# Late queries of branch A projected later, and every other lookup of the first token tile weighed by DVE

## What is computed

```python
n = rms_norm(h, norm1_g) * (1.0 + scale1) + shift1
h = h + gate1 * hybrid_mixer(n)        # three token mixers A, B, C, gated, merged, times w_out
n = rms_norm(h, norm2_g) * (1.0 + scale2) + shift2
h = h + gate2 * peer_ffn(n)            # per token 8 heads x 16 looked-up experts
```

```python
q = rms_norm(q, q_gain); k = rms_norm(k, k_gain)      # q = n @ w_in[:, aq], per head of 64
logits = einsum('bqhd,bqkd->bqhk', q, k_sel) * scale  # k_sel: the top 128 keys by an indexer
p = softmax(where(valid, logits, -inf)); out = einsum('bqhk,bqkd->bqhd', p, v_sel)
```

```python
u = u_tab[expert]; vv = v_tab[expert]                 # 1024 floats each
act = gelu(einsum('nd,nhkd->nhk', xb, u)); out = einsum('nhk,nhkd->nd', g * act, vv)
```

## Time and profile before

| | us |
|---|---|
| median of 3 runs | 2057.0 (2055.41 to 2059.61) |
| the profiled execution | 2055.41 |
| its span, first to last instruction | 2053.6 |
| PE busy | 1667.6 (81%) |
| DVE busy | 1454.6 (71%) |
| ACT busy | 576.0 (28%) |
| POOL busy | 633.5 (31%) |
| DMA moved | 658.7 MB, of which 536.9 MB by the lookups |

### The profile page before, as it was taken

One profiled execution on the slowest core, in us unless ns is written; L12 is line 12 of the kernel. 1 busy time (PEld: TensorE's weight loads), 2 busy tenths in 40 slices (PEclk: granted clock), 3 DMA queues, 4 the chain that ended last, 5 costly groups with the idle time before them and its releaser, 6 DMA issues.

```text
span 2053.6 us, 17698 instructions
## 1 busy us (share of the span) xinstructions
PE 1667.6 (81%) x5546; PEld 926.8 (45%) x5546; DVE 1454.6 (71%) x3352; ACT 576.0 (28%) x1263; POOL 633.5 (31%) x542
## 2 busy tenths in 40 slices
PE   4999999999888898998988667767877676667676
PEld 3443445667777465565655333333443222222222
DVE  5346551668316888887787998877777878887876
ACT  2111122665214442542222223222222222212221
POOL 0000000120002343433334454544444544345441
PEclk8999999999999999999999878888898988788888
DMA  9442120011346999999999999999999999999995
GB/s 372 182 177 96 57 112 30 31 73 51 137 183 277 418 418 420 410 416 407 414 396 420 419 420 379 419 420 419 420 419 420 420 419 420 420 419 420 420 419 240
DMA packets 89806, 658.72 MB, mean 321 GB/s; under 512 B 9952, under 2 KB 11120, under 8 KB 16240
## 3 DMA queue, kind: packets, MB, share of 16 engines
q0 software_dynamic: 73728, 536.90, 63.4%
q1 hardware_dynamic: 14336, 119.18, 14.6%
q10 hardware_dynamic: 1648, 1.51, 0.2%
HBM read 653.95 MB, written 3.34 MB: 320 GB/s over the span
## 4 chain that ended last, share of the span: by engine, by line
DMA 37%; PE 35%; DVE 14%; issue 8%; ACT 4%; POOL 2%; SPq 0%; DVEq 0%; POOLq 0%; PEldq 0%; ACTq 0%
DMA sb<-uv_table,sb 35%; PE ps L1076 10%; PE ps L647 6%; PE ps L649 4%; DVE sb L1959 3%; DVE sb L1983 2%; PE ps L754 2%; POOL sb L2110 2%; PE ps L998 2%; PE ps L959 1%; PE ps L1003 1%; DMA sb<-w_mod 1%; PE ps L926 1%; PE ps L768 1%; PE ps L585 1%
## 5 line engine op out<-in xcount | busy, mean ns | idle before, releaser
L1076 PE MATMUL ps<-sb 128*128 128x512 f32 x1424 | 779.7, 693 | 289.8 <-ACT sb L1453 285.6
L2110 POOL DMA_INDIRECT sb<-uv_table,sb x512 | 606.5, 1185 | 879.8 <-PE ps L1076 663.7
L1959 DVE CUSTOM_DVE_ANT_0 sb<-sb 128x1024 f32<-128x1024 f32 x512 | 625.6, 1222 | 243.2 <-DMA sb<-uv_table,sb 235.7
L1076 PEld LDWEIGHTS ps<-sb 128*128 128x128 f32 x1424 | 294.7, 219 | 720.2 <-ACT sb L1453 413.2
L1453 ACT ACTIVATE sb<-sb 128x128 f32<-128x128 f32 x356 | 132.1, 397 | 601.2 <-DVE sb L1968 590.7
L1983 DVE SCALAR_TENSOR_TENSOR sb<-sb 128x512 f32<-128x512 f32 x304 | 214.8, 748 | 2.2
L1442 ACT ACTIVATE sb<-sb 128x2 f32<-128x2 f32 x256 | 51.7, 202 | 411.6 <-DVE sb L1959 408.3
L2076 POOL TENSOR_TENSOR sb<-sb 128x128 f32<-128x128 f32 x8 | 13.1, 1637 | 435.0 <-DVE sb L1704 435.0
L647 PE MATMUL ps<-sb 128*128 128x512 f32 x304 | 137.8, 606 | 0.0
L959 PE MATMUL ps<-sb 128*128 128x256 f32 (+1 forms) x576 | 114.8, 352 | 0.2 <-DMA sb<-w_pq 0.2
L959 PEld LDWEIGHTS ps<-sb 128*128 128x128 f32 x576 | 97.5, 191 | 28.5 <-issue 17.4
(11 more groups left out here) (267 smaller groups left out, 1773.8 us busy)
## 6 DMA issues: line engine op xcount, KB each, us to landing
sb<-w_mod SPq DMA_DIRECT2D x11, 2048.0 KB, 13.0
sb<-w_pq SPq DMA_DIRECT2D x18, 1152.0 KB
sb<-w_merge SPq DMA_DIRECT2D x24, 768.0 KB
sb<-w_proj SPq DMA_DIRECT2D x8, 2048.0 KB, 8.4
sb<-w_merge SPq DMA_DIRECT2D x6, 2304.0 KB, 9.0
sb<-w_out SPq DMA_DIRECT2D x8, 1024.0 KB, 9.3
sb<-uv_table,sb POOLq DMA_INDIRECT x512, 27.6
sb<-w_merge SPq DMA_DIRECT2D x3, 1536.0 KB, 8.0
```

Source lines behind the costliest of these rows:

```text
L1076: mm = pe.matmul(bank(2 * (t % 2) + f), dgw[m % NDG], row_v(n)[:, T * f:T * (f + 1)], start=(i == 0), stop=(i == PH * PK - 2))
L1959: dve.tensor_tensor_reduce(out=row_u(n), in0=row_u(n), in1=n2_tm(u // PH), scale=1.0, scalar=0.0, op0=ALU.mult, op1=ALU.add, accum_out=dot ...
L2110: pool.indirect_dma_start(out=ring[PLACE[n]], out_offset=None, in_=uv_table, in_offset=bass.IndirectOffsetOnAxis(ap=experts[u % 4][:, i:i ...
```

## The change

**Branch A's late queries.** Jobs 0 to 3 multiply, copy, square, sum and spread only the first 256 columns. The queries of tokens 256 to 511 are projected later by four new PE steps `late_query(0)` to `late_query(3)`, 16 matmul records of 256 columns each: 0 and 1 behind `merge_products(0)`, 2 in slot 0 and 3 in slot 2. Their weights (0.52 MB each) are loaded a second time: 0 and 1 into ring place 7, and 2 into `ya`, ahead of merge 8; 3 when `late_query(2)` is through. ACT copies each pair out with the gain (`late_query_out`), the first pair between `half_gate(0)` and `square(1)`, and squares it; PE sums the squares of a pair per token with eight small matmuls; DVE and ACT make the inverse root of the 8 heads' factors, which now scale the exponentials of the late attention instead of the queries. `kept` no longer holds queries. `merge_products(1)` moves from ahead of the lookups to slot 3. `wo_first` lies in places 3 to 6 and not 4 to 7, so the first lookup into place 3 also waits for `yo_done`, and that into place 7 waits for `late_query(1)`.

**Lookups.** In units 1 to 7 DVE weighs the odd lookups, 8 of 16 where it had 6.

```diff
-        wo_first = ring[4:8]
+        wo_first = ring[3:7]
+        wq_late = [ring[7][:, 0:KT * P], ring[7][:, KT * P:2 * KT * P], area("ya", 2 * T, KT * P), area("ya", 2 * T, KT * P)]
...
         def on_dve(n):
             u, i = divmod(n, PK)
+            if 0 < u < PH:
+                return i % 2 == 1
             return i in ON_DVE or (i in ALSO_DVE and u % PH > 0 and n < 2 * PH * PK)
...
-        EARLY_MERGES = 2
+        EARLY_MERGES = 1
         MERGE_SLOT = {slot: EARLY_MERGES + i for i, slot in enumerate(
-            [4, 7, 8, 11, 12, 15, 16, 19, 20, 22, 23, 24, 26, 27, 28, 29, 30, 31, 32, 33, 34, 35])}
+            [3, 4, 7, 8, 11, 12, 15, 16, 19, 20, 22, 23, 24, 26, 27, 28, 29, 30, 31, 32, 33, 34, 35])}
...
+        LATE_QUERY_AT = {0: 2, 2: 3}
...
                         sp.wait_ge(s["co_done"], 1)
-                        for p in (0, 2, 3):
+                        for p in (0, 1, 3):
                             sp.dma_start(wo_first[p], w_out[:, 2 * KT * P * p:2 * KT * P * (p + 1)]).then_inc(wo_first_in[p], 16)
+                        sp.dma_start(ring[7], w_proj[0][:, 0:2 * KT * P]).then_inc(s["ql_in"], 16)
+                        sp.dma_start(wq_late[2], w_proj[0][:, 2 * KT * P:3 * KT * P]).then_inc(s["ql_in"], 16)
...
             merge_weights(3)
-            merge_weights(4)
+            sp.wait_ge(s["proj_done"], NJ + 3)
+            sp.dma_start(wq_late[3], w_proj[0][:, 3 * KT * P:4 * KT * P]).then_inc(s["ql_in"], 16)
...
                     if kind == "d":
-                        mm = pe.matmul(bank(b), w[:, i, k, :], n_t[:, k, :], start=(k == 0), stop=(k == KT - 1))
+                        n = job_cols(j)
+                        mm = pe.matmul(bank(b, n), w[:, i, k, :], n_t[:, k, 0:n], start=(k == 0), stop=(k == KT - 1))
...
             score(1)
             merge_products(0)
+            late_query(0)
+            late_query(1)
             squares_sum(1)
...
             score(2)
-            merge_products(1)
+            late_query_sums(0)
...
+            def late_query_out(pair):
+                act.wait_ge(s["proj_done"], NJ + 2 * pair + 2)
+                b = bank(3 + 2 * pair)
+                for qt in range(2, TT):
+                    act.activation(q_h(qt)[:, 2 * pair:2 * pair + 2, :], tiles(b, 2)[:, :, P * (qt - 2):P * (qt - 1)], ACT.Copy,
+                                   scale=vcol(V_GAIN))
...
+                act.activation(sq_late, b, ACT.Square).then_inc(s["sq_ready"], 1)
...
             half_gate(0)
+            late_query_out(0)
             square(1)
...
-                act.activation(p, p, ACT.Exp, bias=anmax[:, i:i + 1], accum_out=asum[:, i:i + 1]).then_inc(s["prob_ready"], 1)
+                act.activation(p, p, ACT.Exp, scale=ql_col(j), bias=anmax[:, i:i + 1], accum_out=asum[:, i:i + 1]).then_inc(s["prob_ready"], 1)
...
             variance(1)
+            late_query_var(0)
             dot(4)
             dot(5)
             normed(1)
+            late_query_factors(0)
             weights(2)
-            half_merge(1)
...
-                elif 4 <= PLACE[n] < R_EARLY:
+                elif 3 <= PLACE[n] < 7:
                     pool.wait_ge(s["yo_done"], 4)
+                elif PLACE[n] == 7:
+                    pool.wait_ge(s["proj_done"], NJ + 2)
```

More of the change, by code:

```diff
@@ L424, in job_bank, with job_cols @@
             return j % 4 if j < J_A else {NJ - 3: 6, NJ - 2: 5, NJ - 1: 4}.get(j, 7)
+        def job_cols(j):
+            return H if jobs[j][1] == 0 else T
         J_SMALL = max(i for i, j in enumerate(jobs) if j[0] == "c")
@@ L613, in square_sums, with spread @@
                 sel = area("const", C_SEL + 16 * t, 16)
-                pe.matmul(bank(b, T, 0, 0, 16), sel, sq[i % 2], start=(t == 0), stop=(i in (4, N_STAT - 1)))\
-                  .then_inc(s["sq_used"], 1)
-            def spread(done, i, t):
+                n = H if i < 4 else T
+                pe.matmul(bank(b, n, 0, 0, 16), sel, sq[i % 2][:, 0:n], start=(t == 0), stop=(i in (4, N_STAT - 1)),
+                          skip_group_check=True).then_inc(s["sq_used"], 1)
+            def spread(done, i, t, n=T):
                 sel = area("const", C_SELT + P * t, P, 0, 16)
-                pe.matmul(bank(4 + i % 2), sel, st_r, start=True, stop=True).then_inc(done, 1)
+                pe.matmul(bank(4 + i % 2, n), sel, st_r[:, 0:n], start=True, stop=True).then_inc(done, 1)
             def spread_b(t):
@@ L1023, in output_piece, with late_query, late_query_sums @@
                 mm.then_inc(s["yo_done"], 1)
+            def late_query(i):
+                pe.wait_ge(s["ql_in"], 48 if i == 3 else 32)
+                if i == 2:
+                    pe.wait_ge(s["yg_ready"], 4)
+                w = tiles(wq_late[i], KT)
+                for k in range(KT):
+                    mm = pe.matmul(bank(3 + 2 * (i // 2), H, H * (i % 2)), w[:, k, :], n_t[:, k, H:T],
+                                   start=(k == 0), stop=(k == KT - 1))
+                mm.then_inc(s["proj_done"], 1)
+            def late_query_sums(pair):
+                pe.wait_ge(s["sq_ready"], N_STAT + pair + 1)
+                for t in range(2):
+                    for i in range(2):
+                        mm = pe.matmul(bank(3 + 2 * pair, 2, 4 * t + 2 * i), sq_late[:, H * i + P * t:H * i + P * (t + 1)],
+                                       area("const", C_SEL, 2), start=True, stop=True)
+                mm.then_inc(s["sq_used"], 1)
             def between(t, c):
@@ L1096, in late_turn @@
                     pe.wait_ge(s["tm_out"], 6)
+                    pe.wait_ge(s["stat_var"], 3)
                 for st in range(2 + j // HA + 1):
@@ L1139, in _ @@
                             score(q)
+                if slot in LATE_QUERY_AT:
+                    late_query(LATE_QUERY_AT[slot])
+                if slot == LATE_SQ_AT:
+                    late_query_sums(1)
                 if slot in MERGE_SLOT:
@@ L1195, in project_out @@
                     else:
-                        c = act.activation(o, bank(b), ACT.Copy, scale=scale)
+                        c = act.activation(o, bank(b, w), ACT.Copy, scale=scale)
                     if stat is not None:
@@ L1473, in _ @@
                 diagonals(pair)
-            half_gate(1)
             root(1)
+            late_query_root(0)
             act.activation(warm, cact[:, 0:1], ACT.Gelu)
@@ L1492, in _ @@
                     exponents(u + 1)
+                if slot == LATE_ROOT_AT:
+                    late_query_root(1)
                 if slot in LATE_SUM or part == 1:
@@ L1498, in _ @@
                     scores_out(QUERY_SLOT[slot - 2])
+                if slot == max(LATE_QUERY_AT):
+                    late_query_out(1)
                 if slot in MERGE_SLOT:
@@ L1852, in late_sum, with late_query_var, late_query_factors @@
                 dve.wait_ge(s["pt_done"], i - 1)
-                dve.tensor_tensor_reduce(out=prob_h(j), in0=bank(2, n), in1=pen_h(qt), scale=HD ** -0.5, scalar=-3.4e38,
+                dve.tensor_tensor_reduce(out=prob_h(j), in0=bank(2, n), in1=pen_h(qt), scale=1.0, scalar=-3.4e38,
                                          op0=ALU.add, op1=ALU.max, accum_out=amax_h(j)).then_inc(s["la_read"], 1)
                 dve.wait_ge(s["la_read"], i + 1)
-                dve.tensor_scalar(anmax[:, i:i + 1], amax_h(j), -1.0, None, ALU.mult).then_inc(s["nmax_ready"], 1)
+                dve.tensor_scalar(anmax[:, i:i + 1], amax_h(j), ql_col(j), -1.0, ALU.mult, ALU.mult).then_inc(s["nmax_ready"], 1)
+            def late_query_var(pair):
+                dve.wait_ge(s["sq_used"], N_STAT + pair + 1)
+                dve.tensor_scalar(ql_var[:, 8 * pair:8 * pair + 8], bank(3 + 2 * pair, 8), 1.0, HD * EPS, ALU.mult, ALU.add)\
+                   .then_inc(s["stat_var"], 1)
+            def late_query_factors(pair):
+                c = slice(8 * pair, 8 * pair + 8)
+                dve.wait_ge(s["stat_rt"], 3 + pair)
+                inverse_root(ql_r[:, c], ql_rt[:, c], ql_var[:, c], ql_t[:, c]).then_inc(s["stat_r"], 1)
+                dve.wait_ge(s["stat_r"], 3 + pair)
             def late_out(qt):
```

56 lines of the change are left out of this document (37 added, 19 removed).

## The result

The changed kernel takes 2082.2 us (median of 4 runs, 2078.6 to 2083.7), the kernel before on the same chip 2058.3. Over all runs shared with it the ratio is 1.0118, 95% interval 1.0103 to 1.0133: slower by 24 us where 2056.2 was forecast, and outside the range of 2044 to 2065. Run once more later (e12), it gave 2079.2 (4 runs) and a ratio of 1.0107 (1.0090 to 1.0123).

A forecast was written before the change was run, and what follows sets the result against it. Time saved before 635 us moves the end one for one; after 636 us only bytes and DMA standstills count. Terms -15.2 + 3.7 + 9.5 + 2.0 + 1.25 - 2.0 = -0.75, so median 2056.2 us, range 2044 to 2065.

The forecast's parts named there:

- its own sign of being wrong: DMA engines staying full across the start of the lookups, or GB/s below 410 through the first tile after it.
- head: Projection, jobs 0 to 3 at half width: first spread 13.3 us earlier, four spreads 1.9; -15.2 us, bounds -17 and -11.
- two loads ahead of merge 8: SP's queue: 1.57 MB of late query weights make merge 8 land later, nothing hiding it; +3.7 us, bounds +3 and +5.
- start of the lookups: square(1) waits for late_query(1), ninth lookup at 671.4, DMA bytes last to 663.6; +9.5 us standing still, bounds +5 and +13.
- slots 0 to 3: PE gets 12.4 us more work, place for lookup 16 free near 695, DMA busy to about 693; +2, bounds 0 and +6.
- bytes: Saturated part: 0.52 MB more, late query weight 3; +1.25 us.
- odd rows on DVE: Units 1 to 7, 14 more lookups on DVE: neither PE nor DVE bounds; -2 us, bounds -3.5 and +5.
- rest of the first tile: First token tile outside the other terms: no term of its own in the sum, so 0, and no bounds.
- Rival (c): Head gains 10 and not 15.2, as the earlier projection load delays mod2 loads and DVE paces; 2061.4 us, chance 0.12.
- What can be won is only what the DMA engines lose in that tile: First tile, odd rows on DVE: five slices at 350 to 405 instead of 419 GB/s, 3.5 us; -2 taken.
- the 49 us that its dots waited for rows cover that: First tile: DVE's rise from 279 to 300 of 340 us busy is covered by its waiting for rows.
- rival (b): DVE becomes the bound of the first tile, freeing odd places late; +10 if half is uncovered, 2068 us, chance 0.13.

The follow-up runs named there:

- e12: The changed kernel run once more, unchanged, against the kernel before: 2079.2 us (ratio 1.0107).
- e7: Changed kernel with the old six lookups on DVE, square(1) before late_query_out(0), rest_sum(3) behind the inverse root, two late loads behind merge 8: 2052.6 us (0.9985).
- e3: Changed kernel with ACT's square(1) ahead of late_query_out(0): 2069.2 us (ratio 1.0053).
- e11: e7 with late_query(2) and (3) in slots 1 and 3 instead of 0 and 2, sums of their squares in slot 4: 2049.4 us (0.9957).
- e9: Kernel before with DVE weighing rows 1, 3, 6, 9, 10, 12, 13, 15 in units 1 to 7: 2059.6 us (1.0008).
- e1: Changed kernel with the old rule for DVE's lookups (6 of 16), so the late queries alone: 2070.7 us (ratio 1.0068).
- e8: e7 with merge_products(1) moved from slot 3 to slot 4 and the later ones one place further: 2053.5 us (0.9986).
- e10: Kernel before with DVE weighing rows 1, 3, 5, 9, 11, 15 in units 1 to 7: 2064.2 us (1.0029).
- e6: Kernel before with DVE weighing rows 7, 9, 11, 12, 13, 15 in units 1 to 7: 2066.5 us (1.0032).

## Why the prediction was wrong, point by point

The sum was -0.75 us, profile to profile; it is +28.3. The prediction had named its own sign of being wrong, GB/s below 410 through the first tile; it came, with 382. Term by term:

| term of the sum | forecast | in the traces |
|---|---|---|
| head | -15.2 | -6.9 (after), -13.1 (e12), at the score stage |
| two loads ahead of merge 8 | +3.7 | +3.7 |
| start of the lookups | +9.5 | +9.8 |
| slots 0 to 3 | +2.0 | +8.0 |
| bytes | +1.25 | taken as forecast |
| odd rows on DVE | -2.0 | +7 |
| rest of the first tile | 0 | +4.3 |

The last column adds up to 27.2. Of what is left, 0.9 us lie between the score stage and the first lookup: -6.9 and +3.7 make -3.2, and that lookup is 2.3 us earlier.

**Right.** Merge 8: the wait went from 3.08 to 6.79 us, a difference of 3.71, and e7, which moves the loads, has 2.99:

```profile
575.09 5.50 PE L773 MATMUL ps<-sb 128*128 128x256 f32 x16 [6.79 <-DMA sb<-w_merge]
```

The start: the ninth lookup 38 us after the first, as forecast; the four rows from 656 to 672 us above are 9.8 us short of 419.5 GB/s, 9.5 forecast. e3 shows the chain. The first spread waits for DVE and starts at 93.79 us (94 forecast). Job 5 starts at 68.80 us (68.6 forecast). `late_query(3)` at 691.64 does not wait for its load, asked for at 682.17, which landed 8.2 us later (6 forecast). That does not decide how the queues are served: of the seven lookups asked for since 669.46 and the load itself, 7.9 MB, the DMA engines had moved about 7.4 MB by then, so behind all of them it would have landed about 1 us later.

**The head was over-sized.** The instruction order was right and the clock was taken for granted: all durations came from rows at 1.00, but the step that makes PE wait also makes it less busy, and the next job ran at 0.50 in one execution and at 0.72 in another. The bounds of -17 and -11 hold for e12, not for the execution that was compared. For the median this is some 2 to 8 us of the miss. Rival (c), a head that gains less, came in part, but by the clock and not by a later `mod2` load: that load let `rest_sum(3)` start at 83.41 (83.8 forecast).

**Slots 0 to 3 were under-sized.** 17.8 us stand still from 640 to 720, 9.8 of them at the start. Of the 8.0 that are left, 6.6 lie in 692 to 704 us. There PE does a query and `late_query(3)` in a row, and POOL waits behind both:

```profile
688.08 3.72 PE L978 MATMUL ps<-sb 128*128 128x256 f32 x16
691.64 3.62 PE L1051 MATMUL ps<-sb 128*128 128x256 f32 x16
695.10 5.32 PE L1117 MATMUL ps<-sb 128*128 128x512 f32 x12
```

```profile
697.75 1.42 POOL L2196 DMA_INDIRECT sb<-uv_table,sb  x1 [9.23 <-PE ps L1117]
```

This is lookup 16, and the prediction had listed both pairs of blocks ahead of it; the sizes were wrong. Its terms, from 667.5 on, add up to 696.7 and not to "near 695". With 1.7 us to the data and DMA engines busy to 693 that is 5.4 us, where +2 was put down. (No row showed the 1.7 us; from the issue of lookup 16 to DMA engines that were full again it was about 3 us.) On top of it the six weighings took 13.26 us and not 11.4, at a granted clock of 0.51 and 0.64 in two of the 4 us rows above, and 0.8 us of work in L1131 was not listed. The DMA engines stayed busy some 3 us longer than forecast, which made up for part. e11, in which one late query and not two lies ahead of lookup 16, gives back 3.3 of e7's 9.5 us.

**The odd rows had the wrong sign.** The step that failed is "What can be won is only what the DMA engines lose in that tile", a win of 2 us where the term is a loss of 7. That "the 49 us that its dots waited for rows cover that" held, as far as e9 tells: it has as many rows on DVE, and its loss (1.0008, 0.9999 to 1.0018) is within the noise. So rival (b), given 0.13, named the place (the first tile slows through DVE's rows) but not the mechanism, an overloaded DVE. I priced a choice of rows by its number of instructions. What counts is which rows they are. Among other things the choice decides which engine frees the first row behind PE's block (row 12). The dips were read in the earlier trace rows as something that less work on PE could only mend.

**The rest of the first tile.** e1, with the old rows, still stands still for 4.3 us more than before from 720 to 1000. e7 and e11, in which the tile begins with a shorter stall, have 2.9 and 2.7 us there, fewer than before. That would fit a cause in the state in which the tile starts, but it is not shown: e8, with the same 9.5 us up to 720 as e7, has 6.0, and e3, with a shorter stall at the start than after, has 18.1 and not 15.2. The cause of this term stays open.

The range failed because three terms came out beyond their bounds, all on the same side: slots 0 to 3 (8.0, bound +6), the odd rows (+7, bound +5) and, in the profiled execution, the head (-6.9, bound -11). The rest of the first tile had no bounds at all.

## What to carry to other kernels

Where a ring is freed by two engines in order, look up which engine frees the first place behind each long block, and try to keep that row off the engine that does the block. In these runs the choice of rows cost 7 us of DMA time with six rows on DVE (e10) and 1.7 with eight (e9), so the number alone says little. e6 shows that one such row is not enough. When work is put into a short stretch ahead of a full DMA queue, follow the queue through all the blocks of that stretch and add its terms up again at the end: here the list of blocks was right and its sum was not. And if an edit makes TensorE wait, price the work behind the wait at both clock levels.

## What the runs showed of the hardware

The same program can differ by 6 us at 325 us from one execution to the next (325.40 and 319.29 for the same matmul in the two profiles of the changed kernel). PE's busy time up to there differs by 6.3 us and its idle time by 0.2, and the mean granted clock is 0.91 and 0.93. Sixteen 128x512 matmuls took 9.74 us where the clock was partly at its lower level and 7.15 at the full one.
